# Last tail of a two-layer hybrid decoder step: product banks, panel loads, instruction order and final token ranges changed

## The reference

```python
xp = xp + mp[2] * op                       # op = attention output @ at_wo
hp = pre_norm(xp, norm2_g[i], mp[3], mp[4])
xp = xp + mp[5] * sq_relu_mlp(hp, mlp_up[i], mlp_down[i])
# sq_relu_mlp(h, w_up, w_down) = square(relu(h @ w_up)) @ w_down, hidden width 4096
y_prompt = rms_norm(xp, final_g)           # and the same for the 8 samples
```

## Time and profile before

| | us |
|---|---|
| median of 3 runs (2857.41 to 2865.46) | 2863.49 |
| the profiled execution | 2863.83 |
| its span, first to last instruction | 2862.0 |

### The profile page before, as it was taken

One profiled execution on the slowest core, in us unless ns is written; L12 is line 12 of the kernel. 1 busy time (PEld: TensorE's weight loads), 2 busy tenths in 40 slices (PEclk: granted clock), 3 DMA queues, 4 the chain that ended last, 5 costly groups with the idle time before them and its releaser, 6 DMA issues. The chain is left out here.

```text
span 2862.0 us, 52698 instructions
## 1 busy us (share of the span) xinstructions
PE 2621.4 (92%) x21418; PEld 2462.7 (86%) x21418; DVE 1515.0 (53%) x2879; ACT 1120.1 (39%) x2256; POOL 785.8 (27%) x584
## 2 busy tenths in 40 slices
PE   5989999899688999999999998988878999999997
PEld 3669898888578999999999997877868899999997
DVE  5348786379775212212112536674776655555555
ACT  5447532344354202203113444564445434434333
POOL 1122112023310122222222311012157754444441
PEclk7999999999798999999999999999989999999998
DMA  8868778798741222222221314012112221111112
GB/s 337 305 247 265 245 241 241 201 211 203 222 138 47 99 89 74 89 89 74 90 88 60 119 36 121 20 49 74 42 54 77 89 60 45 45 53 49 49 45 75
DMA packets 379415, 340.16 MB, mean 119 GB/s; under 512 B 115512, under 2 KB 348668, under 8 KB 372238
## 3 DMA queue, kind: packets, MB, share of 16 engines
q1 hardware_dynamic: 348284, 296.27, 33.9%
q10 hardware_dynamic: 25458, 21.57, 2.6%
q0 software_dynamic: 5440, 19.00, 1.8%
HBM read 256.65 MB, written 78.78 MB: 117 GB/s over the span
## 5 line engine op out<-in xcount | busy, mean ns | idle before, releaser
L1324 PE MATMUL t_acc<-t_area,wH 128*128 128x258 f32 (+1 forms) x1536 | 463.5, 302 | 16.0 <-issue 4.5
L1325 PE MATMUL t_acc<-t_area,wH 128*128 128x258 f32 (+1 forms) x1536 | 458.8, 299 | 0.0
L1326 PE MATMUL t_acc<-t_area,wL 128*128 128x258 f32 (+1 forms) x1536 | 458.5, 298 | 0.0
L548 POOL TENSOR_TENSOR wL<-raw,wH 128x1024 fp32r<-128x1024 f32 x62 | 149.1, 2405 | 716.2 <-ACT wH L672 716.2
L1619 DVE SCALAR_TENSOR_TENSOR X<-t_acc,mod,X 128x344 f32<-128x344 f32 (+3 forms) x448 | 237.5, 538 | 144.6 <-PE t_acc L1326 110.0
L1324 PEld LDWEIGHTS t_acc<-t_area,wH 128*128 128x128 f32 x1536 | 294.8, 192 | 18.9 <-issue 10.3
L1325 PEld LDWEIGHTS t_acc<-t_area,wH 128*128 128x128 f32 x1536 | 294.7, 192 | 0.2
L1326 PEld LDWEIGHTS t_acc<-t_area,wL 128*128 128x128 f32 x1536 | 293.9, 191 | 0.0
L569 PE MATMUL t_acc<-twoH,wH 128*128 128x344 f32 x768 | 249.5, 325 | 5.8 <-DVE twoL L891 4.8
L571 PE MATMUL t_acc<-twoH,wL 128*128 128x344 f32 x768 | 246.4, 321 | 0.0
L570 PE MATMUL t_acc<-twoL,wH 128*128 128x344 f32 x768 | 246.1, 320 | 0.0
(11 more groups left out here) (531 smaller groups left out, 6688.1 us busy)
## 6 DMA issues: line engine op xcount, KB each, us to landing
ada_ring<-in_ada_w SPq DMA_DIRECT2D x24, 1024.0 KB, 7.5
shared<-in_ada_w SPq DMA_DIRECT2D x24, 1024.0 KB, 6.3
raw<-in_mlp_up SPq DMA_DIRECT2D x80, 256.0 KB, 2.8
t_plain<-in_mlp_down SPq DMA_DIRECT2D x80, 256.0 KB, 2.6
raw<-in_mlp_down SPq DMA_DIRECT2D x32, 512.0 KB, 4.1
raw<-in_mlp_up SPq DMA_DIRECT2D x30, 512.0 KB, 4.2
kvrb_hx<-hx_saved ACTq DMA_DIRECT2D x16, 516.5 KB, 4.5
kvr_work<-scr_L SPq DMA_DIRECT2D x16, 516.0 KB, 5.7
```

Of the source, the lines that this page charges most:

```text
L548: pool.tensor_tensor(low, raw_of(w), high.bitcast(F32), ALU.subtract).then_inc(s_low, 1)
L1324: pe.matmul(out, high, h, start=begin, stop=False, skip_group_check=True)
L1325: pe.matmul(out, high, l, start=False, stop=False, skip_group_check=True)
L1326: return pe.matmul(out, low, h, start=False, stop=end, skip_group_check=True)
```

## The change

Five things change in `stage_last`, nothing in the other stages.

1. **Loads.** Panels 4 to 7 of `at_wo` get places of their own and are all issued at the start of the stage; ACT copies panels 2 to 7 before anything else. The splits for p = 0 start one block later (table `LOWS`) and the last 14 of 28 are moved behind the jobs P1, P2 and P6 of round 0.
2. **Banks.** P2 gets a bank of its own and is no longer accumulated on P1; in half rounds P6, P7, P5 and P4 each have a bank. The adds move from ACT's relu to DVE (`after`).
3. **Prologue.** Five pairs of groups in half rounds: rounds 0 to 4 with p = 0, rounds 5 to 9 with p = 1, rounds 10 to 20 full. The fills start in round 1, one DVE step behind every second d job and two behind P6, P7 and P5.
4. **Orders.** `rest_of` and `lows_at` say in which order the products and the low parts of the quads come; `BANKS` = (0, 2, 1, 3) says which bank the second product's jobs use, and its first jobs wait for less. The last full round takes its p = 0 products first.
5. **Final ranges** of 430, 344 and 258 tokens; tiles 0 to 5 come between the jobs and 6 to 8 behind them. Odd tiles are scaled by ACT out of PSUM, and POOL multiplies them by the gain.

```diff
-PROLOGUE = 4
+PROLOGUE = 5
-QUADS = ("11", "22", "21", "12")
+BANKS = (0, 2, 1, 3)
+FINAL = ((0, 430), (430, 774), (774, TOK))
...
+    def rest_of(r):
+        if len(rounds[r][1]) == 1:
+            return [(name, rounds[r][1][0]) for name in REST]
+        if r < R - 1:
+            return [(name, p) for name in REST[:3] for p in range(2)] + [(name, p) for p in range(2) for name in REST[3:]]
+        return [("P6", 0), ("P6", 1), ("P7", 0), ("P5", 0), ("P7", 1), ("P4", 0), ("P3", 0), ("P5", 1), ("P4", 1), ("P3", 1)]
+    def lows_at(r, name, p):
...
+        if len(ps) == 1:
+            return {"P4": [(p, "22")], "P3": [(p, "21"), (p, "12")]}.get(name, [])
...
+    HALVES = 2 * PROLOGUE
+    LOWS = {(3, m): (2 * m - 2, 2 * m) for m in range(1, DB)}
+    LOWS_FIRST = {"P1": (14, 20), "P2": (20, 24), "P6": (24, 28)}
-    for r in range(PROLOGUE):
-        fills += [(r, "d", n, 1) for n in range(1, 2 * DB, 2) if r] + [(r, x, 0, n) for x, n in (("P6", 2 if r else 0), ("P7", 2), ("P5", 2), ("P3", 3))]
+    for r in range(1, PROLOGUE):
+        fills += [(r, "d", n, 1) for n in range(1, 2 * DB, 2)] + [(r, x, 0, 2) for x in ("P6", "P7", "P5")]
...
+        def bank_of(r, name, p):
+            if r >= HALVES:
+                return p if name in ("P6", "P7", "P4") else 2 + p
+            return {"P6": 0, "P7": 1, "P5": 2, "P4": 3, "P3": 2}[name]
...
             def out_panel(m):
-                sp.wait_ge(s_olow, m - 3)
-                sp.dma_start(raw[:, m % 2], panel_of(wo, m * 128)).then_inc(s_oraw[m % 2], 16)
+                sp.dma_start(panel_raw(m), panel_of(wo, m * 128)).then_inc(s_oraw[m - 4], 16)
...
                 elif name == "P2":
-                    out = lead[p]
-                    pe.wait_ge(s_p1, n + 1)
+                    out = second(r, p)
+                    if r:
+                        pe.wait_ge(s_r11, turn[before[r, p], p] + 1 if r > HALVES else turn[r, ps[0]])
...
-                    pe.wait_ge(s_c21, turn[s, ps[-1]] + 1)
-                    pe.wait_ge(s_c12, turn[s, ps[-1]] + 1)
+                    pe.wait_ge((s_c21, s_c12)[n % 2], turn[s, ps[0] if n < 2 else ps[-1]] + 1)
...
             def after(u):
...
+                if name == "P2":
+                    dve.wait_ge(s_p1, n + 1)
+                    dve.tensor_tensor(t[1], second(r, p)[:, 0:TQ], first, ALU.add).then_inc(s_r11, 1)
+                    return
...
             def tile(i):
...
+                if s:
+                    act.wait_ge(s_finv, i + 1)
+                    if i >= 2:
+                        act.wait_ge(s_fout[1], 16 * (i // 2))
+                    rows = raw[0:n, 1].rearrange("p k m -> p (k m)")
+                    for h in range(2):
+                        act.activation(rows[:, 512 * h:512 * h + 512], spare[2 + h][0:n], ACT.Copy, scale=root[0:n, 1:2]).then_inc(s_fc, 1)
...
+            for i in range(1, len(TILES), 2):        # on POOL
...
+                for h in range(2):
+                    pool.wait_ge(s_fc, 2 * (i // 2) + h + 1)
+                    c = slice(512 * h, 512 * h + 512)
+                    pool.tensor_tensor(rows[:, c], rows[:, c], fg[0:n, c], ALU.mult).then_inc(s_fy[1], 1)
```

More of the change, by code:

```diff
@@ L1090, in stage_last @@
             weights.append(("p", r, name))
[L1091 to L1095 removed]
+        for name, p in rest_of(r):
+            ends["p", r, name] = len(jobs)
+            jobs.append(("p", r, name, p))
     mids.append((len(jobs), len(jobs) + NT * DB))
@@ L1348, in bank_free @@
                 at, end = mids[r]
-                busy = [u for u in range(at, end) if mid_bank[u] % 4 == n]
+                busy = [u for u in range(at, end) if BANKS[mid_bank[u] % 4] == n]
                 pe.wait_ge(s_add, added[busy[-1]] if busy else 3 * DB + 5 + n)
@@ L1557, in _ @@
                     prepare(q + 1, m)
-                if q == 0 and m < 4:
-                    out_high(4 + m)
-                if q == 3:
-                    for n in range(3 * m, 3 * m + 3):
-                        combined_high(n)
+                for n in range(*LOWS.get((q, m), (0, 0))):
+                    combined_high(n)
                 square(u, m, q)
@@ L1569, in _ @@
                 refill(u)
-            for n in range(24, 28):
-                combined_high(n)
             for u in range(4 * DB, len(jobs)):
@@ L1576, in _ @@
                     ps = rounds[r][1]
-                    if name == "P1":
-                        first_copy(u)
-                        if r and p == ps[0]:
-                            piece_high(r - 1, rounds[r - 1][1][-1], "12")
-                    if name == "P2":
-                        first_relu(u)
-                    if name == "P6" and p == ps[-1]:
+                    if r == 0:
+                        for n in range(*LOWS_FIRST.get(name, (0, 0))):
+                            combined_high(n)
+                    if name == "P6" and p == ps[0]:
                         at, end = mids[r]
@@ L1604, in _ @@
                     if r == R:
-                        t = a // TT
-                        if t == 1 and m in (2, 5):
-                            tile(m // 3)
-                        if t == 2 and m in (2, 4, 6):
-                            tile(1 + m // 2)
-            for i in range(5, len(TILES)):
+                        t = FINAL.index(span)
+                        if t and m in (2, 4, 6):
+                            tile(3 * t - 4 + m // 2)
+            for i in range(6, len(TILES)):
                 tile(i)
@@ L1778, in _ @@
                     token_sum(n)
-                if q == 3:
-                    for n in range(3 * m, 3 * m + 3):
-                        combined_low(n)
+                for n in range(*LOWS.get((q, m), (0, 0))):
+                    combined_low(n)
             add_square(3, DB - 1)
-            for n in range(24, 28):
-                combined_low(n)
             for u in range(4 * DB, len(jobs)):
```

308 lines of the change are left out of this document (157 added, 151 removed).

## The result

The changed kernel takes 2813.09 us (median of 4 runs, 2810.66 to 2816.27) against 2863.11 (4 runs, 2857.41 to 2865.46): ratio 0.9829, 95% interval 0.981 to 0.9848, 50.0 us less. The prediction said 2809.0, in a range of 2786 to 2832. Its own profiled execution took 2810.66 us, with a span of 2807.0.

The account below looks back on a forecast made before the run. PE bounds the last stage, losing time mainly to P2's wait for ACT's copy of P1. Terms -13.4 - 26.0 - 5.0 - 2.1 - 8.8 = -55.3 us from 2863.8 give 2808.5, stated as 2809; range 2786 to 2832.

Parts of the forecast that it names:

- The bound and the whole: Last stage: PE is the bound, its main wait is P2's for ACT's copy of P1; -55.3 us in all.
- Projection: Start of the last stage: earlier panels and residual give -5.0 us, later splits in the last quarter -2.1.
- Rounds 0 to 10: Ten half rounds and one full: 272.1 us after, against 298.1 for the same work before, -26.0 us.
- The late quads of round 4: Work that round 5 takes over from round 4, so round 5 takes 24.0 us.
- Fill rounds: Rounds 1 to 4: DVE decides, its fills stretched beside POOL; 26.6 us a round against 29.6 before.
- The hand count: DVE's order from P6's start in fill rounds: add of P6 at 2.0 us, P3 1.7 us late.
- Full rounds: Ten full rounds: P2's own bank removes 1.34 us each, nothing comes in its place; -13.4 us.
- The end: Behind the last product: no starting wait, three tiles instead of four; 44.7 us instead of 53.5, -8.8 us.
- A: Rival: rounds 1 to 4 stay bound by DVE and POOL at 30.5 us each; 2825 us, chance 0.18.
- B: Rival: fills find POOL idle, 22.5 to 23.5 us a round, round 0's root wait short; 2792 us, chance 0.13.
- C: Rival: POOL and DVE hold each other, PE's clock drops, half rounds 30.5 us; slower, 2875 us, chance 0.03.
- D: Rival: no gain, P2 waits for its weight instead and d jobs for the quads; 2860 us, chance 0.04.

Follow-up runs that it names:

- experiment 2: Changed kernel with P2 again accumulated on P1 in one shared bank in rounds 11 to 20: 2823.54 us, a full round 44.00 us instead of 43.27.
- experiment 7: Changed kernel with the at_wo panel loads in old order behind old waits, ACT's copies beside the first blocks: 2824.16 us, projection 104.2 instead of 99.0.
- experiment 1: Changed kernel with DVE's add of P6 ahead of the two low parts of quad 11 in full rounds: 2810.51 us, a full round 42.77 instead of 43.27.
- experiment 9: Changed kernel with all output tiles scaled by DVE, none through ACT and GpSimd: 2810.83 us, the end 47.7 us instead of 48.4.
- experiment 5: Changed kernel with 56 DVE fill operations of rounds 1 to 4 reading one SBUF tile instead of two: 2812.01 us, these rounds 104.1 instead of 104.5.

## Why the prediction was right, and where it was off

- **The bound and the whole: right.** PE's wait for the copy of P1 was the main loss, and it is gone; in full rounds half of it is the bank's doing (experiment 2), in half rounds the parts of the change were not tried apart. 48.6 of 55.3 us came in the stage; the median is 4 us above the forecast.
- **Projection: right, 1.5 us short.** First quarter -5.0 as predicted (31.5 to 26.5), last quarter -2.8 against -2.1, and 0.8 in the middle. The 5.0 are luck in their make-up: the residual came 12.7 us after the stage's start, where the forecast's 1975 made it 13.8, and job 4 waits 0.2 us, not 1.3; in its place stands job 5's wait of 1.36. The profile puts that one down to GpSimd's panel, but panel 5 was ready at 1967.04; it is for DVE's add of block 1, behind the split of 4.17 us (experiment 7). The forecast had panels early and no price for what GpSimd's run does to DVE.
- **Rounds 0 to 10: right in sum, by errors that cancel, and by a trace at the short end:** six kernels that leave these rounds alone took 272.1 to 277.7 us, so -26.1 against -26.0 is luck, -20.5 to -26.1 what the traces show. Round 0 20.6 (20.1), with the two waits foreseen; round 1 26.1 (27.3); 2 to 4 78.4 (79.8); round 5 21.6 (24.0); 6 to 9 92.8 (88.8). The late quads of round 4, priced at 2.4 us in round 5, did not appear in this trace (other kernels took up to 23.2 there); rounds 6 to 9 took 23.2 on average instead of 22.2: round 6, 24.2, has P2 waiting 1.0 and the first d job 0.4, the others, 22.8 to 23.0, waits of up to 0.5.
- **Fill rounds: mechanism right, place of the price off.** P3 waits 2.3 to 2.9 us, not 1.7. The hand count began with the add of P6 ending at 2.0; DVE and GpSimd in round 2 of after, where P6 starts at 2115.13:

```profile
2116.31 1.32 DVE L1754 TENSOR_TENSOR t_area<-shared,t_area 128x258 fp32r<-128x258 f32 x1 [0.15 <-ACT t_area L1573]
2117.55 0.41 DVE L1767 TENSOR_TENSOR shared<-t_acc,shared 128x258 f32<-128x258 f32 x1
2117.89 1.18 DVE L1718 TENSOR_TENSOR t_plain<-t_plain 128x258 f32<-128x258 f32 x1
...
2121.85 1.49 DVE L1715 TENSOR_TENSOR t_plain<-t_plain 128x258 f32<-128x258 f32 x1
2123.26 0.41 DVE L1774 TENSOR_TENSOR shared<-t_acc,shared 128x258 f32<-128x258 f32 x1
```

```profile
2116.04 4.18 POOL L1325 TENSOR_TENSOR wL<-raw,wH 128x512 fp32r<-128x512 f32 x3 [0.18 <-ACT wH L1499]
2120.18 1.46 POOL L1338 TENSOR_TENSOR raw<-raw 128x512 f32<-128x512 f32 x1
```

  the add of P6 ends at 2.8, since the low part of "11" stands ahead of it, 1.32 us long beside GpSimd. The two fills between the adds of P6 and P7 take 2.5 us, those between P7 and P5 2.6; 1.9 and 2.7 were predicted. What was put behind P3 came out smaller: the first d jobs wait 0.2 us at most, and PE has one wait of 1.5 us later in the d jobs, in round 4. Hence 26.1 us on average against 26.8.
- **Full rounds: the step that failed.** "After the change 10 full rounds ... x 1.34 = -13.4" counted what leaves and asked only POOL what is late next. The count of P2 was right (P1 to the first d job 7.13 to 5.76 us, -1.37). The moved low parts of "11" were not priced on DVE's path to P7: +0.50 a round, 5 us, shown by experiment 1. They fall beside GpSimd's operation there, the lock that the forecast priced in the fill rounds and not here. And about half of the 1.37 was not the bank's (experiment 2), most likely ACT's order, which the sum did not need to know.
- **The end: mis-sized by 3.7 us.** The start without a wait and three tiles at the end came true. X is complete 34.8 us after the last product, not 30.6. The 3.47 us from matmul to matmul around the fourth tile, 2.5 above the 0.95 of the others (experiment 9 has the reason), and DVE's lag of 4.0 behind the last block, not 2.3, were missing: DVE's tile work stands ahead of its adds in program order. The way through ACT and GpSimd, priced as a gain, costs 0.75 us (experiment 9).
- **Rivals.** A (DVE and GpSimd bind the fill rounds at 30.5) did not come: 26.1. B did not: the fill rounds took 25.0 to 26.8, not 22.5 to 23.5, and round 0 20.6. C did not: the clock is 1.00 from round 4 to the last product. D did not, though P2 waits for its weight in rounds 6 and 7, 1.0 and 0.5 us.

## What to carry to other kernels

When a wait goes because work moves to another engine or another place, price the moved work at its new place on every engine's order: here two operations of 0.43 us, moved ahead of an add on DVE and under an operation of GpSimd, took 1.66 us there and ate 5 of 13 us; putting the add first gave them back. A load that comes earlier also moves the work behind it: GpSimd's run on the panels held a DVE operation for 4.17 us. Before giving a value more room (a bank, a buffer), look whether the engine that frees it is idle or busy with work that can wait; if busy, issuing it first may do the same. Spreading work over a stretch that is full on two engines moves the wait and not the time. And before a small difference is put down to an edit, look at how much that part varies in kernels that leave it alone.

## What the runs showed of the hardware

- One DVE operation with a single SBUF input (`tensor_scalar`, 128x258) took 0.28 us with GpSimd idle and 1.0 to 1.4 among GpSimd's operations without a break (experiment 5); the add with an operand in PSUM kept 0.41 in the same stretch.
- Among the d jobs of round 2 of after a DVE fill with two SBUF inputs took 0.42 us beside GpSimd, as with GpSimd idle, and GpSimd's operation of 1.29 took 1.40 to 1.50. Which of the two is held up is not the same everywhere.
- The same GpSimd operation (L1338, L1340, 128x512) took 1.26 to 1.29 us alone, 1.31 to 1.34 beside one-input and 1.45 to 1.47 beside two-input operations of DVE.
- Behind two GpSimd operations of 2.4 us in a row (128x1024, from 1967.01) a DVE operation of 0.43 us, started at 1967.93, took 4.17 and ended only when both had ended.
- Of three pauses of PE of 2.8 to 2.9 us, in rounds 2, 3 and 4 of after, the first was followed by matmuls at 0.21 us start to start, the lower level, from 2125.13 on to 2128.4, which makes the 0.95 of round 3; behind the other two they ran at 0.12. What decides it was not tried.
